# The third mixer of a four-layer block with its tokens stationary and every weight unit split

## The reference

```python
def dilated_diff_mixer(u, w_in, ...):
    dq, dk, dv, fq, fk, fv = jnp.split(u @ w_in, ATTN_SPLITS, axis=-1)   # widths 768 768 768 256 256 256
    dq = rms_norm(dq.reshape(B, S, 12, 64), dil_q_gain)                  # a norm per head
    dk = rms_norm(dk.reshape(B, S, 12, 64), dil_k_gain)
    # three groups of four heads: windows (128,1), (512,4), (2048,16), causal, with ALiBi
    # alpha = softmax of the three groups' log denominators; dil_out = alpha * outs
    fq = rms_norm(fq.reshape(B, S, 4, 2, 32), diff_q_gain)
    fk = rms_norm(fk.reshape(B, S, 4, 2, 32), diff_k_gain)
    # four heads: (softmax(q1 k1) - lam * softmax(q2 k2)) @ v, causal, with ALiBi
    diff = rms_norm(diff, diff_out_gain) * (1.0 - lam_init)
    mixed = jnp.concatenate([dil_out, diff], axis=2).reshape(B, S, 1024)
    return mixed @ w_out
```

## Time and profile before

| | before |
|---|---|
| median of three runs | 2070.2 us |
| the profiled execution: its span | 2069.7 us |
| TensorE busy | 2045.0 us, 99% |
| VectorE busy | 1459.4 us, 71% |
| ScalarE busy | 1250.4 us, 60% |
| chain that ended last | TensorE 91%, VectorE 4%, ScalarE 3%, DMA 1%, issue 1% |
| TensorE clock granted | 9 or more of 10 in all 40 slices |

### The profile page before, as it was taken

One profiled execution on the slowest core, in us unless ns is written; L12 is line 12 of the kernel. 1 busy time (PEld: TensorE's weight loads), 2 busy tenths in 40 slices (PEclk: granted clock), 3 DMA queues, 4 the chain that ended last, 5 costly groups with the idle time before them and its releaser, 6 DMA issues.

```text
span 2069.7 us, 27175 instructions
## 1 busy us (share of the span) xinstructions
PE 2045.0 (99%) x10710; PEld 1708.3 (83%) x10710; DVE 1459.4 (71%) x1193; ACT 1250.4 (60%) x1142; POOL 82.7 (4%) x142
## 2 busy tenths in 40 slices
PE   9999999999999999999999999999999999999998
PEld 9878889788888668889878888888888888888877
DVE  4865546664445645445847888888888889888797
ACT  3654335654437634335655777787778777787674
POOL 1000000100000000000002100000000000000100
PEclk9999999999999999999999999999999999999999
DMA  8427654566644246646336999999999999999997
GB/s 287 143 94 254 236 185 158 180 218 224 207 156 159 80 162 224 223 160 191 120 122 268 408 378 390 363 398 372 389 376 376 384 363 402 363 395 375 382 401 281
DMA packets 211791, 561.27 MB, mean 271 GB/s; under 512 B 10557, under 2 KB 67998, under 8 KB 211566
## 3 DMA queue, kind: packets, MB, share of 16 engines
q1 hardware_dynamic: 204224, 530.61, 70.6%
q0 software_dynamic: 5552, 28.84, 3.5%
q10 hardware_dynamic: 1934, 0.67, 0.1%
HBM read 553.27 MB, written 16.25 MB: 275 GB/s over the span
## 4 chain that ended last, share of the span: by engine, by line
PE 91%; DVE 4%; ACT 3%; DMA 1%; issue 1%; POOL 0%; DVEq 0%; ACTq 0%; SPq 0%
PE ps L2275 15%; PE ps L2277 14%; PE ps L2276 14%; PE ps L666 6%; PE ps L668 6%; PE ps L667 6%; PE ps L536 4%; PE ps L707 3%; PE ps L709 3%; PE ps L708 3%; PE ps L630 2%; PE ps L568 2%; PE ps L545 1%; PE ps L546 1%; PE ps L547 1%; PE ps L2328 1%
## 5 line engine op out<-in xcount | busy, mean ns | idle before, releaser
L2271 DVE TENSOR_TENSOR ring_r<-ring,ring_r 128x2048 fp32r<-128x2048 f32 x336 | 752.9, 2286 | 104.3 <-ACT ring_r L2266 103.9
L2266 ACT ACTIVATE ring_r<-ring 128x2048 fp32r<-128x2048 f32 x336 | 627.6, 1913 | 73.2 <-DMA ring<-in_moe_w_gate 50.0
L2275 PE MATMUL ps<-ring_r,arena_r 128*128 128x512 f32 x1344 | 530.4, 395 | 1.1 <-DVE arena_r L2529 1.1
L2277 PE MATMUL ps<-ring_r,arena_r 128*128 128x512 f32 x1344 | 524.4, 390 | 0.0
L2276 PE MATMUL ps<-ring_r,arena_r 128*128 128x512 f32 x1344 | 524.0, 390 | 0.0
L338 DVE TENSOR_TENSOR ring_r<-ring,ring_r 128x2048 fp32r<-128x2048 f32 x136 | 310.9, 2290 | 218.4 <-ACT ring_r L329 218.4
L329 ACT ACTIVATE ring_r<-ring 128x2048 fp32r<-128x2048 f32 x136 | 259.6, 1913 | 189.0 <-DMA ring<-in_ffn_w_up 77.9
L2277 PEld LDWEIGHTS ps<-ring_r,arena_r 128*128 128x128 f32 x1344 | 252.7, 188 | 54.0
L2275 PEld LDWEIGHTS ps<-ring_r,arena_r 128*128 128x128 f32 x1344 | 252.8, 188 | 52.0 <-issue 1.3
L2276 PEld LDWEIGHTS ps<-ring_r,arena_r 128*128 128x128 f32 x1344 | 253.0, 188 | 50.9
L666 PE MATMUL ps<-ring_r,arena_r 128*128 128x512 f32 (+1 forms) x576 | 216.4, 376 | 1.0 <-DVE arena_r L450 0.8
(11 more groups left out here) (401 smaller groups left out, 2301.2 us busy)
## 6 DMA issues: line engine op xcount, KB each, us to landing
ring<-in_moe_w_gate SPq DMA_DIRECT2D x115, 1024.0 KB, 5.4
ring<-in_moe_w_up SPq DMA_DIRECT2D x112, 1024.0 KB, 6.3
ring<-in_moe_w_down SPq DMA_DIRECT2D x112, 1024.0 KB, 5.3
ring<-in_ffn_w_gate SPq DMA_DIRECT2D x33, 1024.0 KB, 5.0
ring<-in_ffn_w_up SPq DMA_DIRECT2D x33, 1024.0 KB, 5.0
ring<-in_ffn_w_down SPq DMA_DIRECT2D x33, 1024.0 KB, 4.9
ring<-in_attn_w_in SPq DMA_DIRECT2D x24, 1024.0 KB, 5.3
ring<-in_hgrn_w_in SPq DMA_DIRECT2D x16, 1024.0 KB, 5.5
```

Of the source, the lines that this page charges most:

```text
L2266: nc.scalar.activation(unit_parts(k)[0], ring[:, slot_of(k), 0:2048], ACT.Copy).then_inc(m_hi, 1)
L2271: nc.vector.tensor_tensor(low, ring[:, slot_of(k), 0:2048], high, ALU.subtract).then_inc(m_lo, 1)
L2275: nc.tensor.matmul(out_, x[:, 0, f, :], w[0], start=first, stop=False)
L2277: return nc.tensor.matmul(out_, x[:, 0, f, :], w[1], start=False, stop=last)
```

## The change

The third mixer is rewritten; the diff below is cut to its core.

- All twelve MB of the input weights come as halves of 512 columns x 512 rows (`wide_half`), all split. The tokens are stationary for every projection (`quarter(g, t, h)`: group g of 512 columns, token tile t, half h of the rows; 12 matmuls of 512 columns). Groups g: 0 = v of heads 8 to 11 and fq, 1 = fk and v of the differential heads, 2 to 4 = dq and dk, 5 = v of heads 0 to 7. The norm ahead of the mixer now writes split tokens (`HTh`, `HTl`) as the feed-forwards' norms do, and the last feed-forward step also splits the mixer's first unit.
- q and k arrive as tokens x features. ScalarE squares a tile (into `E_sq`) and copies it (`E_raw`), VectorE sums the squares of each head along the free axis (`mean`), GpSimd makes 1/rms with an addition and a power (`E_gpsimd`), VectorE multiplies (`scaled`), TensorE transposes four 128 x 128 blocks (`features`, 8 times), and ScalarE copies them out with the gain. `sum_squares` remains once, for the differential output (`diff_squares`).
- The attention outputs are split (`E_split`), the output units too, and `out(n, f, t)` does one row pair of one unit. Eight such groups of tile 0 are spread among the steps of the head pairs, the rest follows. The results go to banks 0 to 3 (`Y_front`), and the third feed-forward waits for `s_x` ahead of its first up unit.
- The orders of all lists are written anew. Both `E_scalar` and `E_vector` end at unit 17 counted from the mixer's first (units 0 to 11 are inputs, 12 to 15 outputs, 16 and 17 the feed-forward's first two gate units).

```diff
-        E_plan = project(E_w_in, several("F", 2304, 2) + several("H", 2816, 1) + several("F", 0, 6) + several("H", 1536, 3), (3, 4, 5, 6, 7))
-        E_out = project_out(a["attn_w_out_2"][0], (3, 0, 1, 2))
+        E_columns = (2048, 2560, 0, 512, 1024, 1536)
+        E_wide = [[wide_half(E_w_in, c0, h) for h in range(2)] for c0 in E_columns]
+        E_out = project_out(a["attn_w_out_2"][0], (3, 0, 1, 2), raw=0)
...
+            def quarter(g, t, h, part=None):
...
+                    nc.tensor.matmul(o, HTh[:, t, f, :], wh[:, kt, :], start=(f == 0), stop=False)
+                    nc.tensor.matmul(o, HTl[:, t, f, :], wh[:, kt, :], start=False, stop=False)
+                    mm = nc.tensor.matmul(o, HTh[:, t, f, :], wl[:, kt, :], start=False, stop=(f == KT - 1))
+                if part != 0:
+                    if t:
+                        mm.then_inc(w_used, 1)
...
+            def features(x):
+                g, c0 = E_turned_in[x]
+                pe.wait_ge(e_rn, tile_at(g, 1) + 1)
...
+            def out(n, f, t):
+                u, r = E_out[n]
+                if t == 0:
+                    weights_ready(pe, u)
+                    if n:
+                        pe.wait_ge(e_rn, E_low_made(3 * f + n - 1))
+                    else:
+                        pe.wait_ge(e_rn, E_diff_low)
...
+                if t == 0 and (n, f) == (3, 1):
+                    mm.then_inc(s_y, 1)
+                elif t and f:
+                    mm.then_inc(w_used, 1)
...
+            quarter(2, 1, 0), features(1)
+            quarter(2, 1, 1), scores(0)
+            quarter(3, 0, 0), scores(1)
+            quarter(3, 0, 1), features(2), turn(0)
+            quarter(3, 1, 0), features(3), values(0), scores(2)
+            quarter(3, 1, 1), turn(1)
+            quarter(4, 0, 0), values(1), scores(3)
+            quarter(4, 0, 1), features(4), turn(2)
+            quarter(4, 1, 0), features(5), values(2)
+            quarter(4, 1, 1), turn(3)
+            quarter(5, 0, 0), values(3), pair_scores(0)
+            quarter(5, 0, 1), features(6), pair_scores(3)
+            quarter(5, 1, 0), features(7), diff_squares()
+            quarter(5, 1, 1), pair_scores(1), pair_scores(2)
+            out(0, 0, 0)
+            pair_scores(4), pair_scores(5)
+            out(0, 1, 0)
             pair_turn(0)
             pair_turn(1)
             pair_values(0)
             pair_turn(2)
             pair_values(1)
             pair_values(2)
-            keep_busy(6, E_banks[11])
+            out(1, 0, 0)
             pair_turn(3)
+            out(2, 0, 0)
             pair_turn(4)
             pair_values(3)
+            out(3, 0, 0)
             pair_turn(5)
             pair_values(4)
             pair_values(5)
...
+                out(n, 1, 0)
+            for n in range(4):
+                if n == 3:
+                    norm_turn(pe, 5, 0)
+                out(n, 0, 1), out(n, 1, 1)
```

ScalarE's list and VectorE's list, where the prediction walks them:

```diff
+            E_high(7)
+            tile(5)
             exps(0)
-            evac(6)
-            root(4)
             exps(1)
+            features(2)
+            tile(6)
             turned(0)
-            evac(7)
+            E_high(8)
+            features(3)
             output(0)
-            root(5)
+            tile(7)
             exps(2)
             turned(1)
-            evac(8)
+            E_high(9)
...
-            highs_to(act, E_out[3][0] + 1)
+            E_high(17)
...
+            E_low(7)
+            scaled(4)
+            mean(5)
             biased(0)
+            scaled(5)
+            biased(1)
+            mean(6)
             normalised(0)
+            scaled(6)
             normalised(1)
+            E_low(8)
+            mean(7)
             biased(2)
+            scaled(7)
             normalised(2)
+            E_low(9)
             biased(3)
+            mean(8)
+            scaled(8)
             normalised(3)
+            E_low(10)
+            mean(9)
+            scaled(9)
+            pair_biased(0)
+            E_low(11)
+            pair_biased(3)
+            E_low(12)
...
+            pair_biased(1)
+            pair_biased(2)
             greatest(4)
             greatest(5)
...
+            E_low(13)
+            output_low(0)
             normalised(6)
+            output_low(1)
             normalised(7)
-            normalise(8)
-            lows_to(dve, E_out[3][0] + 1)
+            output_low(2)
+            E_low(14)
+            E_low(15)
+            for p in range(3, 6):
+                output_low(p)
+            E_low(17)
```

More of the change, by code:

```diff
@@ new lines, in features @@
+            def features(x):
+                g, c0 = E_turned_in[x]
+                pe.wait_ge(e_rn, tile_at(g, 1) + 1)
+                if x:
+                    pe.wait_ge(e_qn, x)
+                first = c0 if g >= 2 else qk_part(g).start
+                for f in range(2):
+                    for t in range(TT):
+                        mm = nc.tensor.transpose(ps[:, 6, f * SEQ + t * P:f * SEQ + (t + 1) * P],
+                                                 E_raw[:, g % 2, t, first + f * P:first + (f + 1) * P], ident[:, :])
+                mm.then_inc(e_tq, 1)
@@ L1620, in E_tensor @@
[L1620 to L1626, removed]
+            def out(n, f, t):
+                u, r = E_out[n]
+                if t == 0:
+                    weights_ready(pe, u)
+                    if n:
+                        pe.wait_ge(e_rn, E_low_made(3 * f + n - 1))
+                    else:
+                        pe.wait_ge(e_rn, E_diff_low)
+                        pe.wait_ge(e_ev, E_evacuated(11))
+                else:
+                    pe.wait_ge(e_rn, E_low_made(5))
+                wh, wl = (v.rearrange("p (k n) -> p k n", k=2) for v in (slot_hi(u), slot_lo(u)))
+                xh, xl = (v[:, 2 * r + f, t * P:(t + 1) * P] for v in E_split)
+                for c in range(2):
+                    o, cs = ps[:, 2 * t + c, :], slice(c * 512, (c + 1) * 512)
+                    nc.tensor.matmul(o, xh, wh[:, f, cs], start=(n == 0 and f == 0), stop=False)
+                    nc.tensor.matmul(o, xl, wh[:, f, cs], start=False, stop=False)
+                    mm = nc.tensor.matmul(o, xh, wl[:, f, cs], start=False, stop=(n == 3 and f == 1))
+                if t == 0 and (n, f) == (3, 1):
+                    mm.then_inc(s_y, 1)
+                elif t and f:
+                    mm.then_inc(w_used, 1)
@@ L1734, in E_scalar @@
             exps(2)
             turned(1)
-            evac(8)
+            E_high(9)
             output(1)
-            root(6)
             exps(3)
+            features(4)
+            tile(8)
             turned(2)
-            root(7)
-            evac(9)
+            E_high(10)
+            features(5)
             output(2)
             turned(3)
-            evac(10)
+            tile(9)
+            E_high(11)
             output(3)
-            squares(8)
+            act.wait_ge(e_ot, 4)
@@ new lines, in E_scalar @@
+            act.wait_ge(e_ss, 10)
+            nc.scalar.activation(E_sq[0], OT[:, 6:8, :].rearrange("p f t -> p (f t)"), ACT.Square).then_inc(e_ev, 1)
+            features(6)
+            tile(10)
+            E_high(12)
+            features(7)
+            act.wait_ge(e_tq, E_diff_mean)
+            nc.scalar.activation(E_diff_rs, ps[:, 7, :], ACT.Ln, bias=epscol[:, 0:1], scale=1.0 / HD).then_inc(e_qn, 1)
+            act.wait_ge(e_qn, E_diff_ln)
+            nc.scalar.activation(E_diff_rs, E_diff_rs, ACT.Exp, scale=-0.5).then_inc(e_qn, 1)
@@ L1764, in E_scalar @@
             pair_output(2)
+            E_high(15)
             pair_turned(3)
```

353 lines of the change are left out of this document (193 added, 160 removed).

## The result

The changed kernel takes 2098.9 us (median of 4 runs, 2096.8 to 2103.7), the kernel before 2070.6 on the same chip: a ratio of 1.0139, 95% interval 1.0127 to 1.0152. It is slower by 28 us where +12 was forecast, and lies outside the range.

A forecast was written before the change was run, and what follows sets the result against it. TensorE was taken to bound the third mixer nearly everywhere. 24.6 us less work and 4.2 of old waits, against 30.3 and 2.0 of new waits and 8.3 at the handover, gave +11.8: 2082 us, range 2063 to 2092.

The forecast's parts named there:

- the walk: The third mixer's four new engine lists, stepped against each other with measured durations: TensorE waits of 30.3 us before the handover.
- `scores(1)`: TensorE waits 1.4 us for the first bias of `scores(0)`, queued behind E_low(7), `scaled(4)` and `mean(5)`.
- `turn(0)`: TensorE waits 5.4 us for `normalised(0)`, which stands behind `biased(1)` and `mean(6)` on VectorE.
- `values(1)` and quarter (4,0,1): TensorE waits 5.1 us at the two together: a 9.7 us chain against 4.6 of work.
- quarter (5,0,1): TensorE waits 3.3 us because E_low(11) is queued behind `pair_biased(0)`.
- `out(0,0,0)`: First output matmuls wait 5.1 us: the differential heads' low part is behind two pair biases and two `greatest`.
- the handover: Mixer's end: the second gate unit's late DMA holds up the residual; TensorE waits 8.3 us around the next norm's turning.
- 24.6 us less TensorE work: Third mixer: net saving from input, sums of squares, output and `keep_busy`, after 3.6 us added for transposes.
- The rival with a long power: Power on GpSimd takes 4.5 us, so about 9 us more waits in the mixer: 2091 us; chance 0.14.
- TensorE is the bound after all: Rival: nearly all waits in the mixer go, below 5 us left: 2041 us; chance 0.12.
- Half of the waits are absorbed: Rival: one hole gives later steps their lead, taking 15 us off the mixer's waits: 2067 us; chance 0.18.
- The handover doesn't block: Rival: at the mixer's end the gate unit lands before the residual matters, 8.3 us less: 2073.5 us; chance 0.10.

The follow-up runs named there:

- c4: The changed kernel with VectorE's list reordered in four places and nothing else; 2082.6 us.
- c7: The changed kernel with VectorE's four reorderings and both lists of the third mixer ending at unit 16; 2074.1 us.
- c6: The changed kernel with the engine lists rewritten so each chain starts as early as its input allows, and ending at unit 16; 2062.6 us.
- c1: The changed kernel with both lists of the third mixer ending at unit 16 instead of 17; 2090.4 us.
- c8: c6 with the five output groups between the head pairs moved behind `pair_values(5)`; 2066.8 us, ratio 0.9983 to the kernel before.
- c3: The kernel before with one edit: the third mixer's two lists go on to the second gate unit; 2078.8 us.
- c2: The changed kernel with filler matmuls, results unused, in five of TensorE's waits; 2090.3 us.

## Why the prediction was wrong

Direction and the mechanism of the waits were right; the size was less than half, and what was missing has names: the lower clock, put at nothing, and a saving in matmuls put too high. In the mixer's stretch (forecast 156.5 us, measured 171.0):

| term | forecast | measured |
|---|---|---|
| waits of TensorE | 40.6 | 39.0 |
| TensorE work at full clock | 115.9 | about 120.1 |
| lost to the lower clock | 0 | about 11.9 |

The forecast of work is the span's 144.7 less its 4.2 of waits and the 24.6. (The 4.2 is a slip of the prediction: the earlier trace rows have 141.0 us busy and so 3.7 of waits.) The measured split counts half of the time that TensorE is busy at clock 0.50 as lost: 132.0 - 23.8/2. This is an estimate, since not every instruction there need take twice as long, but the kernels agree on it: the same sum gives 120.7 in c4, 120.5 in c7, 120.3 in c6, 119.5 in c1 and 119.3 in c8, while their busy times run from 125.1 to 135.1.

**The waits.** Each step of the walk, forecast and measured: start 1.9 + 0.9, measured 1.6 + 0.8; `scores(1)` 1.4, 2.6; `turn(0)` 5.4, 5.0; `values(1)` and quarter (4,0,1) 5.1, 2.5 + 2.2; quarter (5,0,0) 0.8, 1.2; quarter (5,0,1) 3.3, 3.4; `out(0,0,0)` 5.1, 5.7; `pair_turn(0)` 2.4, 2.1; then 1.0, 1.1, 1.9 against 1.2, 0.7, 1.65; the handover 8.3, 8.0. Only the "short waits" of 2.0 were 0.3. Two of the steps are not the sums of their own terms (`turn(0)` comes to 8.45 - 3.3 = 5.2, `out(0,0,0)` to 4.35), which changes little. c4 shows that they are places in lists: same instructions, 16 us less. c1 and c3 show the handover from both sides.

**The step that failed** is the clock. The prediction read "at full clock throughout" off the kernel before and carried it into a kernel with 39 us of idle TensorE. In this stretch the kernel before had only 3.7 us of idle TensorE in 144.7, no wait over 1.2, and indeed no lower clock. But the same trace shows the fall elsewhere, behind short waits:
```profile
133.46 1.32 PE L463 MATMUL ps<-ident,arena 128*128 128x128 f32 x8 [1.59 <-DVE arena L439]
135.53 0.50 PE L666 MATMUL ps<-ring_r,arena_r 128*128 128x512 f32 x1 [0.75 <-DVE arena_r L450]
...
136.66 0.63 PE L666 MATMUL ps<-ring_r,arena_r 128*128 128x512 f32 x1
137.09 0.63 PE L667 MATMUL ps<-ring_r,arena_r 128*128 128x512 f32 x1
```
```profile
131.50:135.90 4.40, 2.05 (x12) 1.17 (x11) 2.53 (x4) 3.58 (x7) 0.78 (x2) 1.00 1.04 398
135.90:139.30 3.40, 3.40 (x10) 2.66 (x9) 3.40 (x4) 0.43 (x3) 0.00 (x0) 0.50 0.12 41
```
Here the clock fell behind waits of 1.6 and 0.75 us, while waits of 1.6 and 0.8 at the start of the changed mixer (602.1 to 613.0) cost none. The clock row with its 40 slices of 52 us each hides a part of 3.4 us; the table before the prediction (9 or more in all slices) is right and doesn't show it. The prediction's own walk put waits of 5.4, 5.1 and 8.0 us into the mixer, and a lower clock behind them should then have been a rival with a price: at 0.427 us in place of 0.227, one quarter of 12 matmuls costs 2.4 more, and five of them 12. c2 shows the cause: with fillers in the waits, the same matmuls run at 0.23.

**The mis-sized term** is "24.6 us less TensorE work". It was about 20.9 (141.0 before, 120.1 after). Distances taken inside long runs of equal matmuls (0.227) are right there and nowhere else. The first matmul of a quarter is 0.32 us from its next behind transposes (657.34 to 657.66 above), and one quarter among transposes and scores occupies 2.86 us (654.41 to 657.27 in c6), not 2.73; an output group between head pairs 1.50 to 1.58 and not 1.36. Fourteen such quarters and five such groups make about 3 of the missing 3.7 us; the rest has no row.

**The power on GpSimd** was taken as 0.6 us. In the changed kernel, two of its ten rounds, in order of time:
```profile
640.54 2.20 POOL L1862 TENSOR_SCALAR rt<-rt 128x8 f32<-128x8 f32 x1 [6.09 <-DVE rt L1876]
642.83 1.67 POOL L1863 TENSOR_TENSOR rt<-rt,halves 128x8 f32<-128x8 f32 x1
645.98 0.24 POOL L1862 TENSOR_SCALAR rt<-rt 128x8 f32<-128x8 f32 x1 [1.48 <-DVE rt L1876]
646.30 1.65 POOL L1863 TENSOR_TENSOR rt<-rt,halves 128x8 f32<-128x8 f32 x1
```
The power is 1.66 us; a line through this and the 0.57 of one column gives an estimate of 0.4 fixed and 0.16 per column. (The addition is all fixed part: 0.24 for 8 columns, 0.21 for one in the earlier trace rows.) The addition ahead of `scaled(4)` takes 2.20 beside E_low(7) (640.37 to 642.65), as the walk had it. By the lists this made `scores(1)` 2.6 and not 1.4: `mean(5)` and `biased(0)` stand behind `scaled(4)`. Elsewhere it was hidden by the list. The rival with a long power had the duration half right (1.66 of its 4.5) but not the time. Its cost alone was not measured: a kernel with a minimum in its place was planned as the experiment and gave no time.

**The rivals.** "TensorE is the bound after all" needed waits under 5 us; c6, with 13.8, shows what it would have taken, and that the floor is higher than 2041: with no waits and full clock, its profiled execution (2066.0) would be at about 2047. "Half of the waits are absorbed": none was. "The handover doesn't block": it did. Of the signs that the prediction named, the hole before `turn(0)`, the 5 us before the first output matmul and the 8 us before the turning came; 0.227 us in all projections did not.

## What to carry to other kernels

- When lists are executed in order, walk them against each other with measured durations before you believe a saving in matmuls; here a walk of four lists found the waits within 1.7 us in their sum. Then price each wait twice, once as idle time and once as the slower clock behind it: here 39.0 us of waits cost about 11.9 more.
- Look for the lower clock in short windows around the waits. A row of 40 slices over 2 ms doesn't show it.
- An engine that is busy 54% of the time can hold up everything. What counts is whether an item is queued behind something that needs a result not yet there; reordering four places of one list took 16 us off.
- Prefetching "one more unit" at the end of a list is a wait on whoever frees its slot. Ask who frees it, and what stands behind.

## What was not expected of the hardware

- Matmuls behind a wait of 5 us took 0.43 us in place of 0.227, and so did those behind a wait of 2.2 that followed one of 2.5 with 2 us of work between, and in the kernel before those behind waits of 1.6 and 0.75. Fillers of 0.12 us an instruction (28 in 3.29 us ahead of `turn(0)`) kept them at 0.23 there.
- Which matmuls run slow shifts from execution to execution: the wait of 2.6 us at `scores(1)` cost no clock in the changed kernel's profile and did in those of c1, c2, c4 and c7. The changed kernel's four runs spread over 7 us, in the order of their mean clocks (2096.8 at 0.991, 2103.7 at 0.986).
